# Main products of a three-block transformer kernel, with their moving columns and PSUM columns taken from the last to the first

## The reference, cut to what matters

```
for block in (first, second, third):
    h = h + 0.5 * swiglu(rms_norm(h, g1), w_gate, w_up, w_down)   # 1024 -> 2 x 2816 -> 1024
    h = h + mixer(rms_norm(h, gm))                                # projections 1024 -> some 2100 to 3960, back to 1024
    h = h + 0.5 * swiglu(rms_norm(h, g2), w_gate, w_up, w_down)
```

## Time and profile before

| | |
|---|---|
| Median of 3 runs | 1460.78 us (1460.72 to 1460.96) |
| Span of the profiled execution, first to last instruction | 1458.9 us |
| The profiled execution's own time beside its span | not given by the page |
| TensorE matmuls busy | 1452.6 us, 7822 records |
| TensorE weight loads busy | 1250.3 us |
| VectorE busy | 1002.6 us (69%) |
| ScalarE busy | 778.5 us (53%) |
| GpSimd busy | 87.2 us (6%) |
| Transfers | 266.82 MB, mean 183 GB/s |

### The profile page before, as it was taken

How to read it: one execution, slowest core, us unless ns; L and a number is a source line. 1 busy time by engine, 2 the same in 40 slices (tenths; PEclk the granted TensorE clock), 3 DMA queues, 4 the chain that set the end, 5 groups by cost and what they waited for, 6 DMA issues and landing times.

```text
span 1458.9 us, 18627 instructions
## 1 busy us (share of the span) xinstructions
PE 1452.6 (100%) x7822; PEld 1250.3 (86%) x7822; DVE 1002.6 (69%) x1216; ACT 778.5 (53%) x971; POOL 87.2 (6%) x113
## 2 busy tenths in 40 slices
PE   9999999999999999999999999999999999999999
PEld 7888888888888888888888888888888888888887
DVE  6976466787755867459877664787646987687653
ACT  6654355655534555345665544564435876465542
POOL 0000003000000000006100000000000800000000
PEclk9999999999999999999999999999999999999999
DMA  9855563556556555545455556475556543556552
GB/s 328 277 183 178 160 203 116 168 180 201 179 182 202 187 187 189 186 139 172 150 198 188 189 172 206 154 223 182 187 173 217 188 144 118 173 193 205 178 187 72
DMA packets 205620, 266.82 MB, mean 183 GB/s; under 512 B 6944, under 2 KB 148880, under 8 KB 205280
## 3 DMA queue, kind: packets, MB, share of 16 engines
q1 hardware_dynamic: 204320, 261.23, 54.5%
q0 software_dynamic: 1072, 4.35, 0.8%
q10 hardware_dynamic: 144, 0.05, 0.0%
HBM read 264.56 MB, written 1.05 MB: 182 GB/s over the span
## 4 chain that ended last, share of the span: by engine, by line
PE 96%; DVE 2%; ACT 1%; DMA 0%; issue 0%; DVEq 0%; ACTq 0%
PE ps L637 33%; PE ps L643 17%; PE ps L563 14%; PE ps L565 13%; PE ps L564 13%; PE ps L616 1%; PE ps L717 1%; PE ps L812 1%; DVE wlo L1632 1%; PE ps L750 1%; DVE d_i L2025 0%; DVE d_m L2021 0%; DMA G<-in_gains 0%; DVE d_i L2049 0%; PE ps L751 0%
## 5 line engine op out<-in xcount | busy, mean ns | idle before, releaser
L1632 DVE TENSOR_TENSOR wlo<-raw,whi 128x2048 fp32r<-128x2048 f32 (+5 forms) x275 | 567.4, 2068 | 259.0 <-ACT whi L1193 258.6
L1193 ACT CAST whi<-raw 128x2048 fp32r<-128x2048 f32 (+5 forms) x275 | 474.7, 1732 | 222.8 <-PE ps L565 218.4
L637 PE MATMUL ps<-xt,whi 128*128 128x512 f32 x2112 | 511.2, 391 | 0.5 <-DVE xt L2225 0.5
L637 PEld LDWEIGHTS ps<-xt,whi 128*128 128x128 f32 x2112 | 386.0, 188 | 74.4 <-DVE xt L2225 1.3
L643 PEld LDWEIGHTS ps<-xt,wlo 128*128 128x128 f32 x2112 | 274.0, 191 | 12.3
L643 PE MATMUL ps<-xt,wlo 128*128 128x256 f32 x2112 | 277.7, 283 | 0.0
L563 PE MATMUL ps<-whi,xt 128*128 128x512 f32 (+4 forms) x304 | 112.7, 371 | 0.0
L565 PE MATMUL ps<-whi,xt 128*128 128x512 f32 (+4 forms) x304 | 109.7, 361 | 0.0
L564 PE MATMUL ps<-wlo,xt 128*128 128x512 f32 (+4 forms) x304 | 109.5, 360 | 0.0
L563 PEld LDWEIGHTS ps<-whi,xt 128*128 128x128 f32 x304 | 57.3, 188 | 9.2 <-issue 1.0
L565 PEld LDWEIGHTS ps<-whi,xt 128*128 128x128 f32 x304 | 57.2, 188 | 8.5
(11 more groups left out here) (422 smaller groups left out, 1885.8 us busy)
## 6 DMA issues: line engine op xcount, KB each, us to landing
raw<-in_ffn_wi SPq DMA_DIRECT2D x85, 1024.0 KB, 4.9
raw<-in_ffn_wo SPq DMA_DIRECT2D x40, 1024.0 KB, 5.0
raw<-in_ffn_w_gate SPq DMA_DIRECT2D x22, 1024.0 KB, 5.1
raw<-in_ffn_w_up SPq DMA_DIRECT2D x22, 1024.0 KB, 5.2
raw<-in_ffn_w_down SPq DMA_DIRECT2D x20, 1024.0 KB, 4.9
raw<-in_w_in SPq DMA_DIRECT2D x14, 1024.0 KB, 5.1
raw<-in_even_w_in SPq DMA_DIRECT2D x6, 1024.0 KB, 5.2
raw<-in_ffn_wo SPq DMA_DIRECT2D x8, 512.0 KB, 3.8
```

What stands on the lines that cost most here:

```text
L637: return e.matmul(pair.ap[:, b, :], whi[:, v % SPLIT, 256 * j + 128 * b:256 * j + 128 * b + 128], XS[:, j, :, :].rearrange("p h t -> p (h ...
L1193: e.copy(whi[0:n, v % SPLIT, c], raw[0:n, v % RAW, c]).then_inc(s_hi.mark(*[(v, j) for j in js]), 1)
L1632: e.tensor_tensor(wlo[0:n, v % SPLIT, c], raw[0:n, v % RAW, c], whi[0:n, v % SPLIT, c].bitcast(F32), ALU.subtract).then_inc(s_lo.mark(*[(v ...
```

## The change

A new function `backward` issues a matmul with both its moving operand and its output written as a descending slice. Every main product goes through it: the three of `steps`, the three of `last_steps`, the three of `by_tiles`, and `high` and `low` of `wide`. The stationary operand, the waits, the signals, the start and stop flags and the order of the instructions are as before; on every engine the same instructions stand in the same order. The transposes, score, value and recurrence products aren't touched.

```diff
+def backward(e, out, lhsT, rhs, start, stop):
+
+    return e.matmul(out[:, ::-1], lhsT, rhs[:, ::-1], start=start, stop=stop)
...
-                    e.matmul(o, h, hi_w, start=i == 0 and j == 0, stop=False)
-                    e.matmul(o, h, lo_w, start=False, stop=False)
-                    t = e.matmul(o, l, hi_w, start=False, stop=(end or (v == len(plan) - 2 and tt == 1)) and j == nk - 1)
+                    backward(e, o, h, hi_w, start=i == 0 and j == 0, stop=False)
+                    backward(e, o, h, lo_w, start=False, stop=False)
+                    t = backward(e, o, l, hi_w, start=False, stop=(end or (v == len(plan) - 2 and tt == 1)) and j == nk - 1)
...
-                        return e.matmul(pair.ap[:, b, :], whi[:, v % SPLIT, 256 * j + 128 * b:256 * j + 128 * b + 128],
+                        return backward(e, pair.ap[:, b, :], whi[:, v % SPLIT, 256 * j + 128 * b:256 * j + 128 * b + 128],
                                         XS[:, j, :, :].rearrange("p h t -> p (h t)"), start=j == 0, stop=j == 7)
...
-                        e.matmul(pair.ap[:, b, 0:256], wlo[:, v % SPLIT, 256 * j + 128 * b:256 * j + 128 * b + 128],
+                        backward(e, pair.ap[:, b, 0:256], wlo[:, v % SPLIT, 256 * j + 128 * b:256 * j + 128 * b + 128],
                                  XS[:, j, 0, :], start=False, stop=False)
```

More of the change, by code:

```diff
@@ L579, in last_steps @@
                         h, l = (a[:, kt, 128 * tt:128 * tt + 128] for a in (job.act.hi, job.act.lo))
-                        e.matmul(o, h, hi_w, start=tt == 1 and j == 0, stop=False)
-                        e.matmul(o, h, lo_w, start=False, stop=False)
-                        t = e.matmul(o, l, hi_w, start=False, stop=j == nk - 1)
+                        backward(e, o, h, hi_w, start=tt == 1 and j == 0, stop=False)
+                        backward(e, o, h, lo_w, start=False, stop=False)
+                        t = backward(e, o, l, hi_w, start=False, stop=j == nk - 1)
                     names = [("last", tt, c0)]
@@ L600, in by_tiles @@
                         o = pair.ap[:, tt, 0:wd]
-                        e.matmul(o, h, hi_w, start=False, stop=False)
-                        e.matmul(o, h, lo_w, start=False, stop=False)
-                        t = e.matmul(o, l, hi_w, start=False, stop=j == nk - 1)
+                        backward(e, o, h, hi_w, start=False, stop=False)
+                        backward(e, o, h, lo_w, start=False, stop=False)
+                        t = backward(e, o, l, hi_w, start=False, stop=j == nk - 1)
                     if tt:
```

## The result

| | kernel before | changed kernel |
|---|---|---|
| Median | 1460.85 us (4 runs, 1460.72 to 1460.96) | 1482.94 us (4 runs, 1482.52 to 1483.13) |
| Span of the profiled execution | 1458.9 us | 1481.2 us |
| Ratio | | 1.0151 (95% interval 1.0137 to 1.0165) |

A forecast was written before the change was run, and what follows sets the result against it. The prediction took TensorE's stream as the bound and summed span 1458.9 + 0 for columns + 0 for starts, plus 1.9 us around it, to 1460.8 us. Its own range was 1459 to 1463 us, for 8 in 10 1455 to 1505 us.

The forecast's parts named there:

- The bound: Whole kernel: TensorE's stream is the time, matmul side busy 1452.6 of 1458.9 us; no other engine or transfer late.
- The clock, the waits, the consumers: TensorE: granted clock 1.00, waits 3.4 us together; VectorE and ScalarE wait for a group's last product, so see no difference.
- The write side: Results placed in PSUM: columns 511 and 510 share a line, so writing downward changes nothing, 0.424 ns a column.
- the first rival: All 7098 products: columns move singly on read or write side, 0.836 ns each, 2706 us; chance 0.13.
- The price of a column on the read side: Moving operand read from SBUF: a descending column still costs 0.424 ns, so no change.
- The lower bound: Price of a descending column: at least 0.424 ns, as the stream already moves a column in about one clock cycle.
- The two-term model: All 7098 products: time is 0.424 ns a column plus 11 ns a product, 1282 + 78 = 1360 us; neither changes.
- The test I had named: Groups of 512 and 256: equal growth per product blames the start; twice the growth at 512 blames the column.
- the stiffer start: All 7098 products: a stream begins less tightly behind the last, 2 to 6 ns each, 1475 to 1503 us; chance 0.09.
- The sign I had named for a wrong forecast: Profile of the changed kernel: the forecast is wrong if any group of products of one width changes its pace.
- Half pace: All 7098 products: a column costs 0.836 instead of 0.424 ns, adding 1245 us, 2706 us in all; chance 0.13.
- the lost fast form: All 7098 products: two records at 0.836 ns for each column and doubled starts, 5311 us; chance 0.03.

The follow-up runs named there:

- e3_inside: Against the kernel before, all main products take groups of four columns ascending, the four inside each descending, on both sides: 1460.74 us, ratio 1.0000.
- e3_lines: Against the kernel before, all main products take groups of four columns descending, the four inside each ascending, on both sides: 1482.91 us, ratio 1.0152.
- e1_pace: Program of products alone, without the model, widths 128 to 512, ascending against descending read, write or both; 24 products of 512: 5.47 us ascending, 5.61 descending read.

## Why the prediction was right or wrong, point by point

**The bound** was right. TensorE's stream is the time: no wait, transfer or other engine took part in the loss or in the later gain, and 7098 products, of which some took up to 6 ns less or up to 39 ns more, gave -17 to +210 us in the variants.

**The clock, the waits, the consumers** were right: 1.00 in both stretches, four waits of 2.9 us together, nobody late.

**The write side** was right: no change. The Trainium skill's rule ("Advanced Engine Details and Errata", section PSUM Cachelines) taken by its letter would have given the first rival's 2706 us. The write-only kernel ran 1460.92 us, so for a descending run of neighbours the rule doesn't bite.

**The price of a column on the read side** is the step that failed. I wrote that "a descending run by one touches the same pairs and quads of neighbouring elements as an ascending one, only in the other order, and nothing is fetched twice", and concluded 0.424 ns and no change. The first half stands: the order inside a quad is free. The conclusion doesn't: the order in which the quads themselves come isn't free, which is shown by e3_inside (1460.74 us) against e3_lines (1482.91 us). The lower bound was wrong as well, "a direction can't beat that": the descending read gained 1.3 ns at 256 columns, and ascending blocks of 8 gained 6 ns there. ScalarE's row spoke of gaps, never of direction, and said nothing on this.

**The two-term model** failed with it. 0.424 ns a column and 11 ns a product were worked out from two widths, so that both widths "fit the same 11 ns" tested nothing. At 384, 448 and 480 columns the ascending stream of e1_pace takes 175, 203 and 217 ns, 1 to 2 ns more than the two terms give. And I let the rivals change one term or the other. The test I had named, the same growth at both widths or twice the growth at 512, came out as neither: +5.0 ns and -1.3 ns. Of the rivals the stiffer start had the right size (2 to 6 ns a product, 1475 to 1503 us) and the wrong mechanism, since a start that costs would have cost at 256 and 320 columns as well. So the 0.25 for slower and the range up to 1505 us covered the result through a rival whose reason was wrong: that 1482.94 us lies inside the range is luck. The sign I had named for a wrong forecast, a group of one width that changes its pace, came at both widths.

**Half pace and the lost fast form** didn't happen. Where 256 columns are read with a step of 2 or 4, the small program does show the half pace (229 and 233 ns in place of 120), so the pace that the first rival feared exists, for skipped columns and not for a direction. The Trainium skill ("Advanced Engine Details and Errata", section SBUF Cachelines) puts full performance at two hits or more on a 16-byte line; a step of 2 has two and took 229 ns, so for this form the measurement goes against it.

## What to carry to other kernels

Where a stream of products bounds a kernel, read the distance from start to start for each width; a few ns times thousands of products is a per cent that no wait and no busy share shows. The order in which the moving columns are read is free to choose as long as the output follows it, and its price doesn't grow steadily with the width or with the size of the blocks, so it has to be measured for each width. A small program of products alone, which ran 284 us, told the whole kernel's time to 2% of the difference for blocks of 16 and to 3 us for blocks of 8. Don't split a pace into a price per column and one per start from a single order, and then expect another order to change only one of them.

## What the runs showed that was not expected

- Reading float32r columns in ascending blocks of 8 with the 8 reversed makes a product of 256 columns 113 ns instead of 120, and the model 1.15% faster. Blocks of 16 make it 133 ns.
- Fewer stationary columns make an ascending stream of 512 slower: 5.44 us for 24 with 128 of them, 5.52 with 64, 5.57 with 32.
- A plain float32 stream of 256 columns and a bfloat16 stream of 512 have the same pace in both directions.
- At 512 columns descending blocks cost the full 6 to 7 ns a product up to 32 columns and nothing from 64 on.
- Products of 512 columns are slower, by up to 9 ns each for the first five, behind ascending products of 256 than behind products of 256 read in blocks of 8.
- What inside the read makes these paces stays open. A price per jump and a steady price per column are excluded, and fewer bytes of weights beside the descending stream don't speed it up.
